# A two-layer hybrid decoder step: sample tokens turned whole and moved by small transfers, and eight slots for the expert weights

## What is computed

```python
D_MODEL, SEQ, DEPTH, DEC_BATCH, DEC_SEQ = 1024, 256, 2, 8, 8
for i in range(DEPTH):
    h = rmsnorm(x, norm_mix[i])
    z, xbc, dt, q, k, v, g = split(h @ w_in[i])
    xs, Bm, Cm = split(silu(causal_conv(xbc)))         # 16 heads of 64, 2 groups of state 128
    y, ssm = ssd_scan(xs, softplus(dt + bias), -exp(a_log), Bm, Cm, ssm0)   # chunks of 128
    o, ret = retention_chunkwise(rotary(q), rotary(k), v, ret0)             # 4 heads, chunks of 128
    x = x + concat(rms(y * silu(z)), rms(o) * silu(g)) @ w_out[i]
    x = x + cross_attend(rmsnorm(x, norm_mem[i]), mem_k, mem_v)             # 4 heads, 256 memory rows
    x = x + hier_moe(rmsnorm(x, norm_ffn[i]))          # 16 experts, 1024 -> 512 -> 1024, two per token
return rmsnorm(x, norm_final), states, convolution tails, memory projections
```

## Time and profile before

| | |
|---|---|
| median of 3 runs | 1562.76 us (1559.46 to 1563.55) |
| profiled execution, its own time | 1564.11 us |
| its span | 1562.3 us |
| PE / DVE / ACT / POOL busy | 95% / 35% / 17% / 3% |
| mean granted TensorE clock | 0.988 of full speed |
| bytes moved | 395.12 MB |
| chain that ended last, by engine | PE 79%, DMA 15%, DVE 3% |
| expert stage, first pair's gate to last spread, layers 0 and 1 | 548.9 to 778.2, 1320.4 to 1549 us |

### The profile page before, as it was taken

How to read it: one execution, slowest core, us unless ns; L and a number is a source line. 1 busy time by engine, 2 the same in 40 slices (tenths; PEclk the granted TensorE clock), 3 DMA queues, 4 the chain that set the end, 5 groups by cost and what they waited for, 6 DMA issues and landing times.

```text
span 1562.3 us, 19248 instructions
## 1 busy us (share of the span) xinstructions
PE 1480.7 (95%) x8096; PEld 928.9 (59%) x8096; DVE 543.6 (35%) x1152; ACT 264.9 (17%) x587; POOL 46.5 (3%) x78
## 2 busy tenths in 40 slices
PE   7999999899999999998899998998999999999997
PEld 5777668677766734433367776685776666343333
DVE  3323655571123422211324156536511424221222
ACT  1013322130012211001100143211300212100102
POOL 0000000000000000000000000000000000000000
PEclk9999999999999999999999999998999999999999
DMA  8224322885348599999923242328932776999994
GB/s 324 108 108 163 137 98 81 323 329 203 115 181 358 222 373 426 426 427 427 422 76 145 108 160 100 137 95 324 355 115 108 283 295 236 427 425 427 426 427 194
DMA packets 34042, 395.12 MB, mean 253 GB/s; under 512 B 4790, under 2 KB 5238, under 8 KB 9376
## 3 DMA queue, kind: packets, MB, share of 16 engines
q1 hardware_dynamic: 26048, 357.90, 57.2%
q0 software_dynamic: 7904, 35.94, 5.8%
HBM read 369.16 MB, written 27.37 MB: 254 GB/s over the span
## 4 chain that ended last, share of the span: by engine, by line
PE 79%; DMA 15%; DVE 3%; ACT 1%; DVEq 1%; issue 1%; SPq 0%; ACTq 0%
PE psum L580 38%; DMA ring<-stream 14%; PE psum L1185 9%; PE psum L940 9%; PE psum L1205 4%; PE psum L1230 3%; PE psum L596 1%; PE psum L974 1%; PE psum L1019 1%; PE psum L1037 1%; PE psum L990 1%; PE psum L1137 1%; DMA work<-acum_flat 1%; PE psum L587 1%; PE psum L787 1%; PE psum L593 1%
## 5 line engine op out<-in xcount | busy, mean ns | idle before, releaser
L580 PE MATMUL psum<-h,ring 128*128 128x320 f32 x1664 | 456.1, 434 | 0.9 <-issue 0.9
L580 PEld LDWEIGHTS psum<-h,ring 128*128 128x128 f32 x1664 | 313.9, 190 | 134.8 <-issue 7.5
L1185 PE MATMUL psum<-ring,work 128*64 128x512 f32 x768 | 172.6, 594 | 16.4 <-DMA ring<-stream 16.2
L1185 PEld LDWEIGHTS psum<-ring,work 128*64 128x64 f32 x768 | 55.4, 137 | 128.6 <-issue 113.9
L580 PE MATMUL psum<-mem,ring 128*128 128x256 f32 x512 | 122.5, 396 | 6.1 <-DMA ring<-stream 6.1
L580 PEld LDWEIGHTS psum<-mem,ring 128*128 128x128 f32 x512 | 99.1, 197 | 27.8 <-DMA ring<-stream 7.2
L1205 PE MATMUL psum<-work 128*64 128x512 f32 x512 | 113.4, 595 | 1.4 <-ACT work L1592 1.4
L940 PE MATMUL psum<-work,ring 128*128 128x320 f32 x384 | 104.9, 433 | 0.9 <-ACT work L1355 0.9
L940 PEld LDWEIGHTS psum<-work,ring 128*128 128x128 f32 x384 | 72.3, 190 | 30.9 <-ACT work L1355 1.8
L580 PE MATMUL psum<-work,ring 128*128 128x320 f32 x256 | 71.5, 441 | 11.3 <-DMA ring<-stream 10.1
L2121 DVE TENSOR_TENSOR x<-x,psum 128x320 f32<-128x320 f32 x128 | 59.8, 485 | 57.3 <-PE psum L1230 53.7
(11 more groups left out here) (299 smaller groups left out, 1351.6 us busy)
## 6 DMA issues: line engine op xcount, KB each, us to landing
ring<-stream SPq DMA_DIRECT2D x111, 2048.0 KB, 12.3
work<-stream SPq DMA_DIRECT2D x32, 2048.0 KB, 20.6
states_out<-stream SPq DMA_DIRECT2D x24, 2048.0 KB, 15.8
st_out<-states_out POOLq DMA_DIRECT2D x12, 1024.0 KB, 11.1
st_out<-work POOLq DMA_DIRECT2D x6, 1024.0 KB, 8.0
work<-acum_flat POOLq DMA_DIRECT2D x10, 256.0 KB, 3.9
k_mem<-acum_flat POOLq DMA_DIRECT2D x10, 256.0 KB, 3.6
ring<-stream SPq DMA_DIRECT2D x4, 512.0 KB, 8.7
```

Source lines behind the costliest of these rows:

```text
L580: mm = pe.matmul(out, w[:, a:a + P], rhs[:, j, :], start=(j == 0), stop=(j == KD - 1))
L1185: mm = pe.matmul(psum[ab * CAP:(ab + 1) * CAP, up, :], h_packed[:, p % 2, k, ab * CAP:(ab + 1) * CAP], w[:, a:a + BANK], start=(k == 0), s ...
```

## The change

Three things.

**Turns.** The sample tokens are turned as one tile of 64 with one transpose per chunk (t = 2), as the prompt tiles are; the turns of t = 3 and the late ones are gone (19 turns instead of 22). ACT and DVE copy them to a stage in `states_out`, 64 rows, and POOL moves each sample's 8 rows to its partitions by a transfer of its own: 8 each for v and k, 8 for x, 8 for B a layer. v and k move ahead of the scan; the first group's x and B between the broadcasts of steps 1 and 2; the second group's between those of steps 8 and 9, after all projections, since their place is still in what was `h`. DVE, ACT and PE get waits for the moves (`s_moved_v`, `_k`, `_x`, `_b`), and POOL clears the target rows at the start.

**Slots.** `h`, `rstd`, `head_rows`, `conv_tail`, `last_s` and `cbm` become parts of one buffer `rest`, `mem` and `k_mem` of one buffer `store`. In the expert stage both serve as slots 7 and 6. The memory features are loaded again in layer 1.

**h in the expert stage** is no longer written by DVE; the rare case takes it from `h_rows`.

```diff
-WIDER = 6
+WIDER = 8
-    return (2, 3, 0, 1)[(q - Q_OUT) % 4] if q < Q_MOE else (2, 3, 0, 1, 4, 5)[(q - Q_MOE) % WIDER]
+    return (2, 3, 0, 1)[(q - Q_OUT) % 4] if q < Q_MOE else (2, 3, 0, 1, 4, 5, 6, 7)[(q - Q_MOE) % WIDER]
...
+        v_stage = states_out[0:NS, 0, 0:D]
+        x_stage = states_out[0:NS, 0, D:2 * D]
+        k_stage = states_out[0:NS, 1, 1536:1536 + RH * DK]
+        b_stage = states_out[0:NS, 1, 1536:1536 + G * N]
...
@@ sync
+                    if q == SLOTS.index(6):
+                        sp.wait_ge(s_xs, L * 8 + 6)
+                        sp.wait_ge(s_mkstore, 16 * (L + 1))
+                    if q == SLOTS.index(7):
+                        sp.wait_ge(s_rtok, L + 1)
+                        sp.wait_ge(s_quarter, L + 1)
+                        sp.wait_ge(s_tstore, 16 * (L + 1))
...
-                        sp.dma_start(mem[:], mem_in).then_inc(s_mem, 16)
+                    if q == RING - 1:
+                        if L > 0:
+                            sp.wait_ge(freed[6], L * SLOTS.count(6))
+                        sp.dma_start(mem, mem_in).then_inc(s_mem, 16)
@@ tensor
-                if t < 2:
-                    return pe.transpose(out, src[:, cols(t)], ident)
-                for j in range(4):
-                    own = TILE0[t] + j * DS
-                    mm = pe.matmul(out[32 * j:32 * j + DS, :], src[:, own:own + DS], ident, start=True, stop=True,
-                                   skip_group_check=True)
-                return mm
+                return pe.transpose(out[0:TOKN[t], :], src[:, tok(t)], ident)
...
-                for t in range(4):
+                for t in range(3):
                     for half in range(2):
                         turn([zv[:, 4 * half + i, :] for i in range(4)], t)
                 project(Q_Z, range(2, 4))
-                for t in range(4):
+                for t in range(3):
                     turn([kq[:, i, :] for i in range(4)], t)
...
-                        if step == KD - 1:
-                            turn_late(0)
-                            turn_late(1)
...
-                            turn_late(2)
@@ vector
                     if i == 2:
+                        if t == 1:
+                            dve.wait_ge(s_moved_x, 128 * L + 64)
                         times_dt(t + 1)
...
-                        dve.wait_ge(s_lateout, L * 3 + 2)
+                        dve.wait_ge(s_moved_x, 128 * (L + 1))
                         times_dt(3)
...
-                for j in range(KD):
-                    a = PAT["norm_ffn"] + j
-                    dve.scalar_tensor_tensor(out=h[:, j, :], in0=x[:, j, :], scalar=par[:, L, a:a + 1], in1=rstd[:],
-                                             op0=ALU.mult, op1=ALU.mult)
@@ gpsimd
+            def move(dst, stage, gb, moved):
+
+                for j in range(4):
+                    own = (4 * gb + j) * DS
+                    pool.dma_start(dst[32 * j:32 * j + DS, :], stage[own:own + DS, :]).then_inc(moved, 16)
...
+                for i in (4, 5):
+                    pool.wait_ge(s_tout[i % 2], turned_by(L, i))
+                for gb in range(GB):
+                    move(v_of[2 + gb], v_stage, gb, s_moved_v)
+                pool.wait_ge(s_tout[0], turned_by(L, 8))
+                for gb in range(GB):
+                    move(k_of[2 + gb], k_stage, gb, s_moved_k)
                 pool.wait_ge(s_raw_free, L + 1)
                 pool.wait_ge(s_flat, 64 * (L + 1))
...
                     if step == 1:
+                        for i in (14, 17):
+                            pool.wait_ge(s_tout[i % 2], turned_by(L, i))
+                        move(x_of[2], x_stage, 0, s_moved_x)
+                        move(b_of[2], b_stage, 0, s_moved_b)
                         pool.dma_start(conv_out[L], conv_tail[:]).then_inc(s_tstore, 16)
+                    if step == KD:
+                        pool.wait_ge(s_proj, (L + 1) * 45)
+                        pool.wait_ge(s_moved_x, 128 * L + 64)
+                        pool.wait_ge(s_moved_b, 128 * L + 64)
+                        move(x_last, x_stage, 1, s_moved_x)
+                        move(b_last, b_stage, 1, s_moved_b)
```

More of the change, by code:

```diff
@@ L173, in build @@
         x = sb("x", KD, T)
-        h = sb("h", KD, T)
+        rest = sb("rest", 4228)
+        store = sb("store", 2, KD * M)
         work_n = 21572
@@ L205, in view @@
                                **{k: s for k, s in zip(names, shape)})
+        h = view(rest, 0, KD, T)
+        head_rows = view(rest, 2560, 2, T)
+        dt_row, acum_row = head_rows[:, 0, :], head_rows[:, 1, :]
+        squares = head_rows
+        rstd = view(rest, 3200, T)
+        conv_tail = view(rest, 3520, CC, (CW - 1) * (1 + DB))
+        last_s = view(rest, 3844, H, DB)
+        cbm = view(rest, 3972, G, P)
+        mem = view(store[:, 0, :], 0, KD, M)
+        k_mem = view(store[:, 1, :], 0, KD, M)
         zv = view(work, 0, KD, T)
@@ L271, in build @@
         all_w = view(work, 8192, 3, QUAD)
+        h_back = view(work, 8192, 3, D)
         all_in = view(work, 8192, KD, 2, FC, P)
@@ L275, in build @@
         slots = [ring[:, i, :] for i in range(RING)] + [sflat, work[:, 11648:11648 + QUAD],
-                                                        work[:, 11648 + QUAD:11648 + 2 * QUAD]]
+                                                        work[:, 11648 + QUAD:11648 + 2 * QUAD],
+                                                        store[:].rearrange("p a b -> p (a b)"), rest[:, 0:QUAD]]
         some_in = view(sflat, 0, KD, 2, P)
@@ L699, in scores_cb @@
                     mm.then_inc(s_cb, 1)
-                for i in (20, 21):
+                for i in (TURNS - 2, TURNS - 1):
                     pe.wait_ge(s_tout[i % 2], turned_by(L, i))
@@ L1285, in dense @@
                 pe.wait_ge(d_start, L * (E + 1) + 1)
+                pe.wait_ge(d_rows, 48 * (L + 1))
+                for j in range(KD):
+                    if j >= 4:
+                        pe.wait_ge(d_hback, L * KD + j - 3)
+                    for t in range(3):
+                        n = TOKN[t]
+                        mm = pe.transpose(psum[:, j % 4, tok(t)], h_back[0:n, t, j * P:(j + 1) * P], ident[0:n, 0:n])
+                    mm.then_inc(d_hturn, 1)
                 for t in range(3):
@@ L1363, in evac, with turned @@
                     n_evac += 1
-                def turned(dst, width):
+                def turned(dst, width, n=P):
                     nonlocal nt
-                    if nt < 12 or nt % 2 == 0:
-                        act.wait_ge(s_t, L * 22 + nt + 1)
-                        act.activation(dst, psum[:, 4 + nt % 4, 0:width], ACT.Copy).then_inc(s_tout[nt % 2], 1)
+                    if nt < 9 or nt % 2 == 0:
+                        act.wait_ge(s_t, L * TURNS + nt + 1)
+                        act.activation(dst, psum[0:n, 4 + nt % 4, 0:width], ACT.Copy).then_inc(s_tout[nt % 2], 1)
                     nt += 1
@@ L1389, in mixer @@
                 act.drain().then_inc(s_dta, 1)
-                for t in range(4):
+                for t in range(3):
                     for half in range(2):
-                        turned(v_of[t][:, half * BANK:(half + 1) * BANK], BANK)
+                        turned((v_of[t] if t < 2 else v_stage)[:, half * BANK:(half + 1) * BANK], BANK, TOKN[t])
                 for c in range(8):
@@ L1396, in mixer @@
                     if c == 3:
-                        for t in range(4):
-                            turned(k_of[t], BANK)
+                        for t in range(3):
+                            turned(k_of[t] if t < 2 else k_stage, BANK, TOKN[t])
                     for cc in range(c * 3 // 2, (c + 1) * 3 // 2):
@@ L1411, in mixer @@
                             act.wait_ge(s_silu, (L + 1) * CC)
-                        turned(x_of[t][:, half * BANK:(half + 1) * BANK], BANK)
+                        turned((x_of[t] if t < 2 else x_stage)[:, half * BANK:(half + 1) * BANK], BANK, TOKN[t])
                 for t in range(3):
-                    turned(b_of[t], G * N)
-                act.wait_ge(s_t, L * 22 + nt + 1)
+                    turned(b_of[t] if t < 2 else b_stage, G * N, TOKN[t])
+                act.wait_ge(s_t, L * TURNS + nt + 1)
                 b = 4 + nt % 4
@@ L1422, in mixer @@
                 act.wait_ge(s_raw_free, L + 1)
-                def late(i):
-                    act.wait_ge(s_late, L * 3 + i + 1)
-                    dst, src = ((x_last[:, 0:BANK], psum[:, 2, :]), (x_last[:, BANK:], psum[:, 3, :]),
-                                (b_last, psum[:, 1, 0:G * N]))[i]
-                    act.activation(dst, src, ACT.Copy).then_inc(s_lateout, 1)
                 for step in range(10):
@@ L2200, in moe @@
                     dve.drain().then_inc(d_start, 1)
+                    for j in range(KD):
+                        dve.wait_ge(d_hturn, L * KD + j + 1)
```

(1 more changed line is left out.)

83 lines of the change are left out of this document (41 added, 42 removed).

## The result

The changed kernel takes **1569.81 us** (median of 11 runs, 1568.39 to 1579.54), the kernel before 1563.55 beside it (1559.46 to 1568.33): a ratio of 1.0038, 95% interval 1.0024 to 1.0052. It is slower by 0.4%, where I had forecast 1557.8 us. The profiled execution has 1572.81 us of its own time and a span of 1570.6; its mean granted clock is 0.973, against 0.988 before.

What follows compares the result with a forecast made beforehand. PE is busy 95%, but late weight loads bound the expert stage and waits the mixer. Terms -3.6 - 0.8 + 7.4 - 5.5 = -2.5 us a layer, -5.0 for both: 1557.8 us on the median's scale, range 1546 to 1568.

Steps and rivals of the forecast that it cites:

- Turns of v and k: Layer start, ahead of the Z projections: fewer, whole-column turns save 3.6 us a layer, ends -2.0 and -4.1.
- my end of -4.1: The largest saving allowed for the turns of v and k, in us a layer.
- Turns of x and B: Mixer, from the turns of x: shorter turns save 0.8 us a layer, ends 0 and -0.9.
- the broadcast leaves at start + 9.3: Mixer: despite eight moves ahead of it, step 2's broadcast leaves 9.3 us after the turns of x start, as before.
- my end of 0: The least saving allowed for the turns of x and B: none.
- E to retention: From the eighth gate projection's end: step 9's broadcast leaves late behind eight moves, +7.4 us a layer, ends +2.1 and +10.
- The first rival: Step 9's broadcast lands as if alone and the clock holds: +2.1 instead of +7.4 a layer, 1547 us; chance 0.27.
- Expert stage: Loads 42 and 43 go out earlier without a pause, saving 5.5 us a layer, ends 0 and -5.7.
- the third rival: Expert stage: loads 42 and 43 don't move up and the pause stays, +3.0 us a layer, 1569 us; chance 0.09.
- a little late: Expert stage: the allowance for the first gather's lateness, taking the saving from 5.7 to 5.5 us.
- the part on the rule: Expert stage: queues share the DMA engines packet by packet, so two more loads don't delay the rows their full 9.8 us.
- The second rival: Expert stage: rows land after loads 42 and 43, PE stands 6.0 us for pair 1's gather, 1568 us; chance 0.14.

Runs made afterwards that it cites:

- turns_only: The changed kernel with six slots in the expert stage again, memory features loaded once, turns and moves kept: 1571.41 us, ratio 1.0036 to the kernel before.
- bc9_first: The changed kernel with the broadcast of step 9 issued ahead of the eight late moves: 1552.74 us, ratio 0.9923 to the kernel before.
- bc9_mid: As bc9_first, but the broadcast of step 9 also waits for the eighth gate projection: 1561.52 us, ratio 0.997 to the kernel before.
- loads_behind_rows: As bc9_first, but SP holds loads 42 and 43 until the rows for the gathers are ready, not written: 1552.96 us, ratio 0.9925.
- rows_sp: As bc9_first, but SP instead of POOL writes the rows for the gathers, between loads 40 and 41: 1553.16 us, ratio 0.9927.
- hold_loads: The changed kernel with loads 42 and 43 held until the rows for the gathers are written: 1572.75 us, ratio 1.0047 to the kernel before.
- slots_only: The kernel before with only the buffers, the eight slots and the reload of the memory features; old turns, no moves: 1562.75 us, ratio 0.9983.
- six_bc9: As bc9_first, but with six slots in the expert stage: 1557.98 us, ratio 0.995 to the kernel before.

## Why the prediction was wrong

**Turns of v and k, -3.6**: right, a little small. -4.5 (without the 0.8 at the start of the span) and -4.2. I had taken off 0.5 for ACT, which emptied the banks beside PE without a loss; both are at my end of -4.1 or past it.

**Turns of x and B, -0.8**: wrong in sign. From their start to E it is 55.8 us instead of 54.1 in layer 0, and 57.1 in layer 1, so +1.6 and +3.0. The step that failed is "the broadcast leaves at start + 9.3, which is where it leaves now". It did leave at start + 9.4. But I held this against the old time, not against PE, which came to the y of step 1 1.3 us earlier after the start of the turns and therefore stood longer, 3.37 instead of 2.21 us, and lost clock behind it. A saving in front of a fixed wait isn't only lost, it lengthens the stand. The loss itself is the clock: in layer 0 of turns_only, with a stand of 3.40 us behind which the clock held (4.58 us), this stretch took 54.1 us, as before. That is my end of 0, and which of the two comes is chance as far as these runs show.

**E to retention, +7.4**: right in place, mechanism and size. The broadcast left at E + 4.2 as forecast, was read at E + 11.3 (forecast E + 10.6), PE stood 7.8 us (7), the clock fell (2.4 us; 2.7), retention came at E + 28.2 (27.7): +7.8. In layer 1 it was +6.6. bc9_first, bc9_mid and the changed kernel set in a row show that it is this broadcast, and that the load in front of it counts, as I had taken it. The first rival, that it costs little, falls.

**Expert stage, -5.5**: this is the step that failed the forecast, with 4.6 of the 6.7 us a layer by which the sum was off; it measured -0.8 and -1.0. Loads 42 and 43 moved up as I had it, and the third rival falls. My words for the gather were "a little late"; it left 12.5 us after the first gate instead of 3.8, and the unpacking came 23.2 us after it instead of 15.9, plus the clock. The mistake lies in the part on the rule. I argued from gathers that land in 11.2 us beside loads of 20.6 that POOL's queue gets its share, so the two more loads would do no harm. Sharing was right, but the size of the share was the question: a gather is 0.52 MB, the rows are 1.31, and as long as the loads last the rows got 62 of 427 GB/s, a seventh. Two more loads prolong that time: from the first write's issue to the last landing it is 21.3 us instead of 13.7, 7.6 more for 9.8 us of loads. A rule that says "packet by packet" asks for the sizes of the packets, and these stand on the page.

**The second rival**, slower because the first gather comes late, is what happened: 0.6 us gained in the stage (measured 0.8 and 1.0), PE standing 6.0 us (7.11), a fall of the clock, 1568 us (1569.81). Its reason, though, service strictly in the order of issue, isn't what the runs show: the rows are there at 566.2, before load 43 (568.5), which was issued before them, and in loads_behind_rows the order of issue changes nothing. That its price comes so close is in part luck. I had given it 0.14, against an argument I could have checked by one division.

So the sum was -3.6 - 0.8 + 7.4 - 5.5 = -2.5 a layer, with two terms wrong, the turns of x and B by 3.1 and the stage by 4.6; in the traces it is -4.4 + 2.3 + 7.2 - 0.9, +4.2 with the mean of both layers for each term and the E to retention of layer 1 at +6.6; the medians give 3.1. The net over both layers hung on one late wait at each end, and both ends were in one queue, POOL's.

## To carry to other kernels

When small transfers are added to a queue, look at what stands behind them there and when its reader needs it; put them behind the last urgent one: here that turned +0.4% into -0.8%. Before more loads are sent ahead, see which small-packet transfer of another queue must pass them, and put it into the loads' own queue at its place: here that shortened the stage by 3.2 to 3.9 us a layer (rows_sp against bc9_first), while issuing most of it first changed nothing (loads_behind_rows) and holding the loads until it had landed gave the gain away again (hold_loads). A saving in front of a wait that doesn't move is worth nothing, and less than nothing if the stand it makes longer brings the clock down.

## What the hardware showed that I had not expected

The clock doesn't fall behind every stand of one length. Ahead of the y of step 1, PE stood 3.33 us in bc9_first and the projection behind it took 4.57 us; it stood 3.43 us in rows_sp, with the same instructions on all engines up to there, and it took 6.78:

```profile
194.90 4.57 PE L613 MATMUL psum<-rest,ring 128*128 128x320 f32 x16
```

```profile
195.41 6.78 PE L621 MATMUL psum<-rest,ring 128*128 128x320 f32 x16
```

It is no threshold in the length either: the clock fell behind stands of 2.30 us (slots_only, 6.00 us behind it) and 3.30 (six_bc9, 6.27) at this place, and held behind 3.40 (turns_only, 4.58; hold_loads, 4.57). There are three or four such stands a layer, each worth about 2 us or nothing. This alone moves one execution against the next by several us. The profiled executions of rows_sp and bc9_first, with spans of 1549.3 us both, come out alike in this way: 7.2 us less in the two stages, 5.6 more in the scans, 2.0 more between the layers. Whether the runs behind the medians divide in the same way isn't shown, since each kernel has one trace.

The same write of rows lands in 7.3 us on SP's queue, with load 40 in flight ahead of it and three loads behind, and in 13.1 to 17.9 us (medians of the large and the small writes) on POOL's beside four. In these runs POOL's small packets are slow beside SP's large ones for as long as the large ones last, whichever was issued first.
